# Expert weights reordered in memory so that each partition's four rows are one 16 KB run

## What is computed

```python
cap = EC_CAPACITY_FACTOR * n // N_EXPERTS            # 64 latent rows, 16 context rows per expert
aff = jax.nn.softmax(jnp.einsum('bnd,de->bne', h, router_w).astype(F32), axis=-1)
gate, idx = lax.top_k(jnp.swapaxes(aff, 1, 2), cap)
xe = jax.vmap(lambda hb, ib: hb[ib])(h, idx)         # each expert takes its own rows
hid = jax.nn.silu(jnp.einsum('becd,edf->becf', xe, wg)) * jnp.einsum('becd,edf->becf', xe, wu)
ye = jnp.einsum('becf,efd->becd', hid, wd) * gate[..., None].astype(h.dtype)
...at[ib.reshape(-1)].add(yb.reshape(-1, d))         # and adds its results to them
```

## Time and profile before

| | us |
|---|---|
| three runs, median (lowest to highest) | 2185.11 (2178.64 to 2187.02) |
| the profiled execution, its own time | 2176.78 |
| its span, first to last instruction | 2174.6 |
| busy: PE / DVE / ACT / POOL | 1913.6 / 561.2 / 513.1 / 457.1 |
| PE from the first down of a layer to its last (15 experts), layer 0 / layer 1 | 494.83 / 494.95 |

### The profile page before, as it was taken

One profiled execution on the slowest core, in us unless ns is written; L12 is line 12 of the kernel. 1 busy time (PEld: TensorE's weight loads), 2 busy tenths in 40 slices (PEclk: granted clock), 3 DMA queues, 4 the chain that ended last, 5 costly groups with the idle time before them and its releaser, 6 DMA issues.

```text
span 2174.6 us, 41201 instructions
## 1 busy us (share of the span) xinstructions
PE 1913.6 (88%) x17147; PEld 993.8 (46%) x17147; DVE 561.2 (26%) x1103; ACT 513.1 (24%) x1256; POOL 457.1 (21%) x411
## 2 busy tenths in 40 slices
PE   2799998893999999999839999979839999999994
PEld 1455786452344444443325558854514444444441
DVE  0240677234011011010113327743231101101101
ACT  0211554111221221221212125522212212212121
POOL 0130756000111111111102236720001111111112
PEclk8899998995899999999969999979869999999997
DMA  9400300932699999999980030027229999999995
GB/s 357 157 1 8 156 1 1 344 118 104 246 401 394 395 401 394 395 402 394 395 323 20 0 147 17 1 115 289 99 106 384 398 395 397 398 395 401 395 394 212
DMA packets 152902, 540.99 MB, mean 249 GB/s; under 512 B 13490, under 2 KB 21344, under 8 KB 152768
## 3 DMA queue, kind: packets, MB, share of 16 engines
q1 hardware_dynamic: 123088, 481.82, 55.9%
q0 software_dynamic: 13568, 25.96, 5.0%
q10 hardware_dynamic: 16160, 32.10, 4.2%
HBM read 513.33 MB, written 29.26 MB: 250 GB/s over the span
## 4 chain that ended last, share of the span: by engine, by line
PE 68%; DMA 17%; DVE 4%; ACTq 3%; issue 2%; SPq 2%; ACT 1%; POOLq 1%; POOL 1%; DVEq 0%
PE PS L617 21%; DMA ring<-in_exp_w_up 14%; PE PS L625 11%; PE PS L511 6%; PE PS L481 5%; PE PS L450 4%; PE PS L419 4%; PE PS L391 3%; PE PS L392 3%; PE PS L464 3%; ACTq L707 2%; PE PS L393 2%; SPq L274 1%; DMA arena<-x_rows 1%; DMA ring<-in_w_mod 1%
## 5 line engine op out<-in xcount | busy, mean ns | idle before, releaser
L617 PE MATMUL PS<-ring,arena 128*32 128x512 f32 x6144 | 684.2, 596 | 19.6 <-DMA ring<-in_exp_w_up 10.6
L617 PEld LDWEIGHTS PS<-ring,arena 128*32 128x32 f32 x6144 | 195.3, 110 | 446.1 <-issue 402.0
L625 PE MATMUL PS<-ring,arena 128*32 128x256 f32 x6144 | 349.1, 379 | 0.0
L625 PEld LDWEIGHTS PS<-ring,arena 128*32 128x32 f32 x6144 | 199.2, 110 | 173.3 <-issue 57.5
L1458 POOL DMA_INDIRECT x_rows<-arena x64 | 102.5, 1601 | 673.1 <-DVE arena L1277 623.1
L925 ACT ACTIVATE arena<-PS,modB,modA 128x64 f32<-128x64 f32 x272 | 84.0, 414 | 423.3 <-PE PS L604 423.3
L511 PE MATMUL PS<-ring,H 128*128 128x512 f32 x320 | 139.2, 593 | 1.7 <-ACTq L692 1.7
L1444 POOL DMA_INDIRECT arena<-xn_rows,arena x68 | 68.0, 1001 | 315.7 <-DVE arena L1263 296.5
L1317 POOL TENSOR_SCALAR stat<-stat 128x1 f32<-128x1 f32 (+2 forms) x45 | 13.2, 293 | 487.6 <-ACT arena L898 235.7
L481 PE MATMUL PS<-arena 128*128 128x64 f32 x816 | 108.7, 274 | 1.6 <-DVE arena L1125 1.5
L450 PE MATMUL PS<-arena,H 128*128 128x512 f32 x192 | 103.1, 618 | 6.8 <-POOL H L1377 5.0
(11 more groups left out here) (203 smaller groups left out, 1929.7 us busy)
## 6 DMA issues: line engine op xcount, KB each, us to landing
ring<-in_exp_w_gate SPq DMA_DIRECT2D x64, 2048.0 KB, 19.3
ring<-in_exp_w_up SPq DMA_DIRECT2D x64, 2048.0 KB
ring<-in_exp_w_down SPq DMA_DIRECT2D x64, 2048.0 KB
ring<-in_w_mod SPq DMA_DIRECT2D x24, 2048.0 KB, 17.5
ring<-in_w_in SPq DMA_DIRECT2D x8, 2048.0 KB, 20.2
arena<-x_rows ACTq DMA_DIRECT2D x25, 512.0 KB, 6.0
ring<-in_w_out SPq DMA_DIRECT2D x4, 2048.0 KB
x_rows<-arena ACTq DMA_DIRECT2D x10, 512.0 KB, 2.6
```

Source lines behind the costliest of these rows:

```text
L617: last = mm(PS[64 * c + r:64 * c + r + LANE, bank, :], left[:, c0 + r:c0 + r + LANE], ring[:, s0 + k // 4, k % 4, c * HALF:(c + 1) * HALF] ...
L625: last = mm(PS[32 * j:32 * j + 32, bank, 0:QUART], left[:, c0:c0 + 32], ring[:, s0 + k // 4, k % 4, j * QUART:(j + 1) * QUART], start=(k = ...
```

## The change

The host stores each expert matrix already in the order in which the partitions take it: [layer, expert, half, partition, 4 rows, 1024]. The load then reads its half as it lies, so that a partition's four rows are one run of 16 KB in memory as well as in the ring. w_mod, w_in and w_out keep the old layout; their rearrange moves from `slot_load` to `matrix_load`. What PE reads from the ring is the same, element by element.

```diff
             def slot_load(l, rnd, s, src):
                 sp.wait_ge(slot_used[s], l * ROUNDS + rnd + CREDIT)
-                sp.dma_start(ring[:, s, :, :], src.rearrange("(k p) n -> p k n", p=P)).then_inc(slot_ready[s], 16)
+                sp.dma_start(ring[:, s, :, :], src).then_inc(slot_ready[s], 16)
...
-                        slot_load(l, rnd, 2 * m + h, source[l, h * 512:(h + 1) * 512, c0:c0 + D])
+                        slot_load(l, rnd, 2 * m + h, source[l, h * 512:(h + 1) * 512, c0:c0 + D].rearrange("(k p) n -> p k n", p=P))
...
-                            slot_load(l, 3 + e, 2 * m + h, ins[w][l, e, h * 512:(h + 1) * 512, :])
+                            slot_load(l, 3 + e, 2 * m + h, ins[w][l, e, h, :, :, :])
...
+        if name.startswith("exp_w_"):
+            a = np.asarray(a).reshape(2, 16, 2, 4, 128, 1024).transpose(0, 1, 2, 4, 3, 5)
```

## The result

The changed kernel takes 2346.0 us, the median of six runs (2340.9 to 2352.6), against 2185.6 for the kernel before on the same chip: 1.0744 times as long, with an interval of 1.072 to 1.0768. Forecast were 2489 us and a range from 2393 to 2760. The direction and the mechanism were right; the size was not, and the time lies 47 us under the range.

A forecast was written before the change was run, and what follows sets the result against it. PE and the DMA engines were taken as close limits, the scatter-gather loop becoming the bound: 32.56 - 3.2 + 11.8 us plus 2.2 of clock gives 43.4 an interval; 2176.8 - 989.8 + 1302.0 = 2489.0 us, range 2393 to 2760.

The forecast's parts named there:

- The limits and the loads: Expert stage: PE wants 32.56 us an expert; larger pieces cut the DMA engines' need from 33.6 to 32.5 us.
- the limit under the other two: Expert stage: loop from down through scatter, rows_added and gather, 3.2 us to spare, lies under the PE and DMA limits.
- One piece to a turn: DMA queues in the expert stage: each small q0 packet waits for one whole q1 piece, 0.634 instead of 0.164 us.
- The number of turns: Loop's scatters and gathers: 26 turns per engine, all meeting long pieces, adding 11.8 us an interval.
- the stretch from 2190 to 2390 us: Whole kernel: the outcome of a mild slowdown, given a chance of 0.03.
- the upper case: Whole kernel: upper end of the likeliest case, 2573 us, with 2.8 us of cover and 4 us of clock.
- The clock: PE after its stall in the expert stage: restart at lower clock costs 2.2 us an interval, bounds none to 4.
- The queue ahead of the first packet: Rival, scatter and gather: wait before the first packet grows by 7 us if counted in pieces; 2702 us, chance 0.14.
- Small packets: Rival, DMA engines: small packets get in between, the loop keeps its 3.2 us; 2163.8 us, faster, chance 0.10.
- The point of decision: Rival of small packets let in: a delay per turn of 0.12 us, a piece of some 7 KB, decides.
- what was to be shown: Expert-stage signs: quarter of q1's packets, scatters after 12 us or more, gathers 8 to 10, L604 waits, intervals 41 to 46.

The follow-up runs named there:

- gate and up alone: Kernel before with only gate and up matrices loaded in 16 KB pieces, down as before: 2175.5 us, ratio 0.9965 to the kernel before.
- down alone: Kernel before with only down matrices loaded in 16 KB pieces, gate and up as before: 2217.9 us, ratio 1.0157 to the kernel before.

## Why the prediction was wrong in size

**The limits and the loads: right.** The loop through scatter and gather was named as the limit under the other two, with 3.2 us to spare. Growths of 2.8 us (8 KB) and some 3.2 (gate and up alone, the second gather) fitted in 22 and 23 of the 30 intervals, one of 4.5 (down alone, 18.0 against 13.5) did not. A 16 KB piece was put at 0.634 us. Over one interval of the changed kernel:

```profile
q1 hardware_dynamic: 867, 12.63, 81.0%
```

0.810 x 37.6 us x 16 engines = 487 us for 12.63 MB, which are 771 pieces: 0.632 us. That faster loads bring PE to 32.56 us an expert is shown with 8 KB pieces and the early gather; with 16 KB the loop or the gather was late in every kernel here, so it is not shown for that size.

**One piece to a turn: right.** Where q1 is supplied, 17.0 long pieces per engine pass beside the scatters' 18 turns, and the two halves of the change lengthen scatter and gather each by itself. The Trainium skill, DMA: Bandwidth & Descriptors, section "Queues, rings and completion order", lets a queue drain a packet of typically 9 to 17 descriptors before the next has its turn; these counts do not agree with that, and the measurement decides.

**The number of turns: the step that failed.** The forecast said "The loads keep q1 supplied for all of it" and counted 26 turns, each 0.47 us longer. They don't. The slots are let go by PE, which is itself held up by the stall, and gate's load is issued only at 913.84. q1, then q0, in the first scatter, 908.2 to 914, and in the second, 914 to 917.6:

```profile
q1 hardware_dynamic: 137, 1.98, 81.8%
q0 software_dynamic: 131, 0.26, 24.1%
...
q1 hardware_dynamic: 89, 1.20, 79.5%
q0 software_dynamic: 156, 0.13, 23.4%
```

In the first it is nearly one for one, as forecast; in the second q1 has 73 long pieces (1.20 MB) for 128 packets of q0 and the ends of both scatters. The gap itself can be seen: from 916.4 to 917 us down's loads have ended, gate's pieces are only starting, and 74 packets of q0 pass beside 7 long pieces (0.11 MB).

```profile
q0 software_dynamic: 74, 0.07, 72.7%
q1 hardware_dynamic: 21, 0.11, 49.1%
```

Over both scatters, 12.7 long pieces per engine were met, not 18. In the gathers it was 99 or 6.2, not 8 (6 of the 8 turns are data; whether the two completion packets waited for a piece was not separated); q1 while these move, 923.4 to 926.7 and 926.7 to 928.2 us:

```profile
q1 hardware_dynamic: 69, 1.13, 79.8%
...
q1 hardware_dynamic: 46, 0.49, 79.6%
```

18.9 x 0.634 - 26 x 0.164 = 7.7 us instead of 11.8 makes an interval of 32.56 - 3.2 + 7.7 + 2.2 = 39.3 us and a total of 2176.8 - 989.8 + 30 x 39.3 = 2366, within 1% of the measured time: the miss is this term. That it comes so close is partly luck, since the pieces were counted in one of the shorter intervals, whose scatters grew by 4.0 us and not by the 5.1 of the count. In others the gap comes later. In the interval that starts at 814.04, where first scatter to second gather takes 20.0 us, 251 long pieces or 15.7 per engine are met from 829.7 to 841.3 us:

```profile
q1 hardware_dynamic: 283, 4.11, 84.3%
```

The early release of gate's slot confirms it from the other side: there the pieces do come in time, 17.0 per engine, and the way from first scatter to second gather has a mean of 20.4 us, close to the forecast's 21.6. The sum by turns still comes out about 1 us too long in the scatters of both kernels (5.1 against 918.04 - 903.15 - 10.9 = 4.0 us). The queues' shares of the engines add up to over 100%, so their packets overlap a little, but they did so before the change too (53.9 and 52.5% in the earlier trace rows); where this 1 us goes stays open. The mistake in method: the supply of q1 was checked as a total (30.4 us of loads in the time up to 42 us), and that total has a gap in it. No bound was set on the count of turns, only on the price of each, and so the range was too narrow downwards; the stretch from 2190 to 2390 us, where the time came out, had been given a chance of 0.03. Two slips in the working do not bear on this: the gap between the two scatters is 0.6 us by the times beside it (721.4 - 720.8), not 0.4, and the terms named for the upper case add up to 2554 us (32.56 - 2.8 + 11.8 + 4 = 45.6 an interval), not 2573.

**The clock: right, and 0.4 us too large.** 2.2 us an interval were taken; the rows of down and of transposes show 1.3 + 0.5 us, and what the parts leave over is 1.8. That is less than a third of the 6 us by which the 28 intervals grew, so the clock is not the larger part. The stretch from down to down has a clock of 0.95 where the earlier trace rows has 1.00. In the first 3.5 us of its down, after PE had waited 3.16 us in front of `turn_lat`, the clock is 0.55, which is nearly all the time at the lower of its two levels (1.2 GHz):

```profile
892.81:930.43 37.62, 34.47 (x400) 13.91 (x404) 3.75 (x8) 6.88 (x21) 5.18 (x4) 0.95 0.90 357
...
892.74:896.20 3.46, 3.46 (x21) 1.00 (x24) 0.42 (x1) 3.46 (x14) 0.00 (x0) 0.55 1.01 431
```

**The rivals.** The queue ahead of the first packet did not grow: from a scatter's issue to its first packet it is 4.9 us before and 5.0 after, and 4.2 in both for the first gather. So it is bytes or time, not pieces. Small packets are not let in between long pieces. The point of decision given there, a piece of some 7 KB, was nearly right: 8 KB just pass. Of what was to be shown, q1's packets and the landings of the gathers came as named. The scatters landed after 11.5 and 11.8 us in the interval shown and after 12.1 and 12.6 in the mean of the 28, just at the 12 or more that were named. The wait at L604 is there, but with 4.1 us in the mean (132.4 less 12.4 ahead of the layers' first experts, in 29 waits) instead of 8.6. The DMA share was 0.90 in the interval shown and 0.87 and 0.86 over the 15 intervals of each layer, not 0.8, and the intervals took 38.6 us instead of 41 to 46.

## What to carry to other kernels

The piece length of a bulk load also sets the time that every small packet of another queue may wait per turn, so before lengthening pieces find the loop of small transfers that runs beside them, count its turns per engine, and compare the growth with its spare time. A turn only costs when the bulk queue has something to send at that moment: look at the queue's bytes in just that window, not at its total. Here a middle size, 8 KB, had most of the gain and little of the loss, and cutting the loop by issuing the gather earlier removed what was left of the loss.

## What was not expected of the hardware

Giving the loads a slot 3.4 us sooner made the kernel 2.6% slower with 16 KB pieces and changed nothing with 4 KB: an idle moment of the bulk queue was what let the small packets through. Between a scatter's issue and its first packet lie 4.9 to 5.0 us under load with either piece, a wait whose cause is left open. And 56 instructions more in the body of PE's loop over two experts (28 matmuls and their weight loads) brought a stall of 5.7 us before a gate at every turn of the loop, and 128 more instruction packets; the two appeared together, and which caused which was not tested.
